# One more k-pair of Down in seven products, and Up's groups twice as wide

## The chip, the cores and the metric

The kernel runs on one core of a Trainium2 chip. The metric is the time of one execution on the device in microseconds (us). Its engines are TensorE (PE in the profile; PEld is its weight load), VectorE (DVE), ScalarE (ACT), GpSimd (POOL) and SyncE (SP), which here only issues transfers. On-chip memory is SBUF; TensorE writes its sums to eight banks of PSUM, each 128 partitions by 512 numbers.

## The reference

One layer of a trunk over 256 tokens of 2048 numbers, all in float32. The part in question is the last one, the feed-forward block:

```
h   = RMSNorm(x)                      # 256 x 2048
u   = h @ w_up                        # 2048 x 11264, called Up here
u   = sum(conv_w[j] * shifted(u, j) for j in range(3)) + conv_b
a,b = split(u, 2, axis=-1)            # 5632 columns each
x   = x + (silu(a) * b) @ w_down      # 5632 x 2048, called Down here
```

Before it stand another norm, the input projection (2048 x 5632), windowed attention, a gated linear recurrence and the output projection.

## The kernel before

**Three products for one.** Each float32 operand is cut in two parts for TensorE: a high part (a cast to fp32r, by ScalarE) and a low part (the operand less its high part, by VectorE). A product of tiles is high x high, high x low and low x high. Every weight therefore passes a transfer, a cast on ScalarE and a subtraction on VectorE before TensorE can use it. The weights move in units of 128 x 1024 numbers through rings of four buffers (`raw`, `w_hi`, `w_lo`); four units are a "quad". `units_split` counts the units that VectorE has finished, `units_used` those that TensorE has used.

**Up.** The 11264 columns are taken in 44 groups of 256, alternately of the a half and the b half (`for g in range(22)`: a, then b). One group is one quad of weights; TensorE runs 64 matmuls for it, 32 of 512 columns and 32 of 256, into two banks (`quad_channels`). While TensorE runs the next group, ScalarE and VectorE work on the last one (`a_work`, `b_work`): VectorE brings it from the banks to `U` (`evacuate`: two reductions and a product with the norm), ScalarE makes the last tap of the convolution (`last_tap`), VectorE the other two (`taps`), ScalarE the silu of an a group; for a b group VectorE forms the product a*b, ScalarE casts it to `gated`, and VectorE subtracts. Between these steps both engines cut the four units of the next quad (`make_hi`, `make_lo`). Everything runs in the order written, on each engine.

**Down.** The 5632 rows of `w_down` are taken as 22 k-pairs of 256 rows, and the 2048 output columns as two column pairs of 1024. One k-pair of one column pair is a product of 2 x 2 blocks, and with two token tiles it takes eight block products, each of three matmuls: 24 matmuls of 512 columns (`four`). Or it takes seven block products, 21 matmuls, by a scheme in the manner of Strassen and Winograd (`seven`). This needs four sums of weight blocks and four sums of activations. The strings in `PATTERNS` say for each column pair which k-pairs are of which kind: S is seven products, C, D and c are eight. The k-pairs of kind S are the first 16 of the activations (`SEVENS`); the order in which they are taken is `SEVEN_ORDER`.

**The sums.** The sums of activations are made in Up, in the work on a b group, for the groups below `SEVENS` (four small additions on VectorE, then two casts and two subtractions). Fourteen of them stay in SBUF; the rest is written from ScalarE's queue to DRAM (`park_sums`) out of one place at the end of `gated`, and brought back in Down (`fetch_sums`). `hi_of_sums(g)` may write that place again only when the transfer before has landed (`sum_parked`). Of the sums of weights two are built in DRAM ahead of time by GpSimd's queue, with transfers that add, at a pace set by `SUM_STEP` and `FIRST_SUM_UNIT` (one step for each 3.5 units used, from unit 20). A third one is either built there too (for the k-pairs in `THIRD_SUM_IN_DRAM`, 5 of 16) or made by VectorE in Down (L1745); the fourth always by VectorE (L1746).

**Buffers in Down.** The first four k-pairs (kind C) still use the ring of Up. From the fifth on, called q4 here (q counts the 44 k-pair turns of Down from 0), the pieces of a k-pair go through slots: 3 large raw slots and a small one (`slots_in_turn`), and two for the high parts (`HI_SLOTS`), so VectorE can be two turns ahead of TensorE at most. A k-pair of kind S has three pieces: a (two blocks), b (three blocks), c (two blocks). VectorE's order per turn is: cut a, form the sums, cut b, cut c. When the sevens of a column pair are done their banks are merged with the output (`free_the_banks`, `rest_of_merge`, `add_last`, all on VectorE).

Of the kernel before, what the change touches and what calls it, by code (L numbers as in the profile page):

```python
# [31 lines left out]
F32 = mybir.dt.float32  # L32
# [35 lines left out]
UP_GROUPS = D_FF // GC  # L68
OUT_GROUPS = D_MODEL // GT
# [12 lines left out]
PATTERNS = ["CCCCSSSSSSSSDSSSSSSSSc", "CcSSSDSSSSSSSDSSSSSSCc"]  # L82
# [6 lines left out]
THIRD_SUM_IN_DRAM = (1, 4, 7, 10, 13)  # L89
LAST_PARKED_TURN = 6  # L90
# [25 lines left out]
SUM_STEP = (7, 2)  # L116
FIRST_SUM_UNIT, SUM_PAUSE = 20, (30, 38)
# [13 lines left out]
def hybrid_layer(nc, x, attn_norm, w_in, q_norm, k_norm, sinks, lb_logits, hg_norm, w_out,  # L131
                 ffn_norm, w_up, conv_w, conv_b, w_down, out):
    ctx = ExitStack()
    with ctx:
# [26 lines left out]
        eps = sb("eps", [P, 1])  # L161
        N_SMALL = 2 * HG_HEADS + 3 + 2 * KT
        N_CONV = 2 * D_FF // P
        cols = sb("cols", [P, N_SMALL + (1 + CONV) * N_CONV])
# [3 lines left out]
        qk_gain = sb("qk_gain", [P, 1])  # L168
        q_eps = sb("q_eps", [P, TT])
        q_scale = sb("q_scale", [P, 2, TT, 2])  # L170
        ss = sb("ss", [P, TT])
        ss_part = sb("ss_part", [P, TT, OUT_GROUPS])
        x_rms_row = sb("x_rms_row", [P, SEQ])
        neg_ss = sb("neg_ss", [P, TT])
        o_ss = sb("o_ss", [P, TT * 2])
# [35 lines left out]
        small = region("small_region", 8448)  # L211
# [9 lines left out]
        C = sb_at(place, "C", [P, 2, 2, SEQ])  # L221
# [168 lines left out]

        bank_x = [bank[4], bank[5], bank[6], bank[7], bank[1], bank[2], bank[3], bank[4]]
# [119 lines left out]
        sums_of = [[bank[4], bank[5], bank[6], bank[7]], [bank[0], bank[1], bank[2], bank[3]]]  # L511
# [25 lines left out]
        SUMS_BACK_AT = [5, 7]  # L537
        X2_BACK_AT = [[5, 14, 17, 20], [13, 15, 17, 19]]
# [17 lines left out]
        def _(sp):  # L556
# [53 lines left out]
            with sp.Fori(0, UP_GROUPS) as g:  # L610
                load_channels(g * 2 + Q_UP, w_up_v, g * GC)
                load_channels(g * 2 + Q_UP + 1, w_up_v, g * GC + D_FF)
# [168 lines left out]
        def _(act):  # L781
# [76 lines left out]
            def spread_row(n):  # L858
                act.wait_ge(row_spread, n + 1)
                act.copy(x_rms_row[:, :], bank[6][:, 0:SEQ]).then_inc(row_made, 1)  # L860
# [234 lines left out]
            make_hi(Q_UP + 1, 3)  # L1095

            def last_tap(n, ab, g):

                act.wait_ge(groups_evacuated, n + BANK_PAIRS + G_UP + 1)
                for c in range(2):  # L1100
                    col = g * 2 + ab * (N_CONV // 2) + c
                    act.activation(C[:, ab, c, :], U[:, c, 2:SEQ + 2], ACT.Identity,  # L1102
                                   scale=cols[:, bass.ds(col + conv_col(2), 1)],
                                   bias=cols[:, bass.ds(col + C_BIAS, 1)]).then_inc(tap2, 1)

            def a_work(g, quad):
                make_hi(quad, 0)
# [1224 lines left out]
```

## Time and profile before

| | us |
|---|---|
| median of 3 runs | 1080.18 (1080.04 to 1081.68) |
| the profiled execution | 1080.29 |
| its span, first to last instruction | 1078.6 |
| around the span | 1.7 |
| Up, by TensorE's rows | 366.9 to 857.1 |
| Down, by TensorE's rows | 857.1 to 1075.2 |

| engine | busy us | share of the span |
|---|---|---|
| PE | 1073.7 | 100% |
| PEld | 928.9 | 86% |
| DVE | 908.6 | 84% |
| ACT | 633.9 | 59% |
| POOL | 79.8 | 7% |

The granted clock of TensorE is 1.00 over the whole span. The page lists busy time and the chain that ended last; the lists by line and shape give mean durations; the timeline gives starts, from which the step from one instruction to the next on an engine can be read. That step can be shorter than the duration, since an instruction begins before the one before it has wholly ended. Times within the span are counted from its start.

### The profile page before, as it was taken

What the parts mean: (1) busy time and instruction counts of PE and PEld (TensorE: products, weight loads), DVE (VectorE), ACT (ScalarE), POOL (GpSimd) and SP (SyncE); (2) the same over time, 40 slices, a digit from 0 to 9 for tenths busy, and PEclk for the clock granted to TensorE, in tenths of its full rate; (3) what the DMA queues carried; (4) which work ended last, traced back from release to release, by engine and by line L of the source; (5) the groups of instructions that cost most, each with busy time, mean ns of one, the idle gap of its engine ahead of it and who ended that gap; (6) DMA issues with size and microseconds to landing.
All of it is one profiled execution on the core that took longest, in us unless ns stands there. A gap on an engine that the chain in (4) does not pass through costs nothing.

```text
span 1078.6 us, 18188 instructions
## 1 busy us (share of the span) xinstructions
PE 1073.7 (100%) x6543; PEld 928.9 (86%) x6543; DVE 908.6 (84%) x1376; ACT 633.9 (59%) x930; POOL 79.8 (7%) x114
## 2 busy tenths in 40 slices
PE   9999999999999999999999999999999999999998
PEld 9888888888888889888888988888888888888887
DVE  7878988889655678888888888888877889999997
ACT  7677676757554655545555555545555566656663
POOL 4500000000000000000000000000000000000000
PEclk9999999999999999999999999999999999999999
DMA  8656687777889888798888888889888789798884
GB/s 275 183 163 176 190 229 223 216 223 222 234 258 245 278 236 235 240 256 239 249 232 243 237 255 245 227 258 247 271 240 235 218 282 319 256 309 315 260 289 163
DMA packets 192336, 260.77 MB, mean 242 GB/s; under 512 B 9605, under 2 KB 143894, under 8 KB 192022
## 3 DMA queue, kind: packets, MB, share of 16 engines
q1 hardware_dynamic: 176246, 216.24, 62.4%
q0 software_dynamic: 13344, 38.80, 17.6%
q10 hardware_dynamic: 2688, 5.00, 1.2%
q8 instruction: 31, 0.51, 0.2%
q14 instruction: 27, 0.22, 0.1%
HBM read 255.02 MB, written 43.78 MB: 277 GB/s over the span
## 4 chain that ended last, share of the span: by engine, by line
PE 99%; DMA 1%; DVE 0%; SPq 0%; issue 0%; DVEq 0%
PE bank L1821 38%; PE bank L1829 20%; PE bank L2216 7%; PE bank L2215 7%; PE bank L2214 7%; PE bank L2067 3%; PE bank L1868 3%; PE bank L2068 3%; PE bank L2069 3%; PE bank L1869 3%; PE bank L1870 3%; PE bank L1789 1%; PE bank L1897 1%; DMA xt<-in_x_dram 1%; PE bank L2106 0%; PE bank L1986 0%
## 5 line engine op out<-in xcount | busy, mean ns | idle before, releaser
L792 ACT CAST w_hi<-raw 128x1024 fp32r<-128x1024 f32 x299 | 311.9, 1048 | 252.7 <-PE bank L1829 118.4
L1201 DVE TENSOR_TENSOR w_lo<-raw,w_hi 128x1024 fp32r<-128x1024 f32 x299 | 363.8, 1222 | 108.1 <-ACT w_hi L792 107.5
L1821 PE MATMUL bank<-hs,w_hi 128*128 128x512 f32 x1792 | 423.0, 391 | 0.0
L1821 PEld LDWEIGHTS bank<-hs,w_hi 128*128 128x128 f32 x1792 | 331.3, 188 | 66.2 <-issue 0.9
L1829 PEld LDWEIGHTS bank<-hs,w_lo 128*128 128x128 f32 x1792 | 224.6, 192 | 5.7 <-issue 0.2
L1829 PE MATMUL bank<-hs,w_lo 128*128 128x256 f32 x1792 | 227.3, 283 | 0.0
L1171 ACT CAST hi_slot<-slot 128x1024 fp32r<-128x1024 f32 (+1 forms) x102 | 117.7, 1187 | 64.7 <-DVE slot L1746 25.2
L1728 DVE TENSOR_TENSOR slot_lo<-slot,hi_slot 128x1024 fp32r<-128x1024 f32 (+1 forms) x102 | 136.7, 1388 | 5.8 <-ACT hi_slot L1171 4.7
L2216 PE MATMUL bank<-hi_slot,gated 128*128 128x512 f32 (+1 forms) x194 | 75.1, 387 | 0.0
L2214 PE MATMUL bank<-hi_slot,gated 128*128 128x512 f32 (+1 forms) x194 | 75.1, 387 | 0.0
L1646 DVE SCALAR_TENSOR_TENSOR C<-U,cols,C 128x256 f32<-128x256 f32 x176 | 73.3, 478 | 0.0
L2215 PE MATMUL bank<-slot_lo,gated 128*128 128x512 f32 (+1 forms) x154 | 59.5, 386 | 0.0
L1102 ACT ACTIVATE C<-U,cols 128x256 f32<-128x256 f32 x88 | 48.1, 594 | 13.2 <-DVE U L1212 13.2
L1868 PE MATMUL bank<-w_hi,mix 128*128 128x512 f32 x128 | 50.3, 393 | 0.0
L2067 PE MATMUL bank<-w_hi,hs 128*128 128x512 f32 x128 | 50.3, 393 | 0.0
L2068 PE MATMUL bank<-w_lo,hs 128*128 128x512 f32 x128 | 49.9, 390 | 0.0
L1870 PE MATMUL bank<-w_hi,mix 128*128 128x512 f32 x128 | 49.9, 390 | 0.0
L1869 PE MATMUL bank<-w_lo,mix 128*128 128x512 f32 x128 | 49.8, 389 | 0.0
L2069 PE MATMUL bank<-w_hi,hs 128*128 128x512 f32 x128 | 49.8, 389 | 0.0
L2214 PEld LDWEIGHTS bank<-hi_slot,gated 128*128 128x128 f32 x194 | 36.4, 188 | 7.5
L2216 PEld LDWEIGHTS bank<-hi_slot,gated 128*128 128x128 f32 x194 | 36.4, 188 | 7.3
L771 POOL DMA_DIRECT2D u_sums<-in_w_ffn_down_dram x21 | 19.3, 918 | 219.9 <-PE bank L1821 92.3
(248 smaller groups left out, 1183.8 us busy)
## 6 DMA issues: line engine op xcount, KB each, us to landing
raw<-in_w_ffn_up_dram SPq DMA_DIRECT2D x176, 512.0 KB, 5.2
u_sums<-in_w_ffn_down_dram POOLq DMA_DIRECT2D x58, 512.0 KB, 6.7
raw<-in_w_in_dram SPq DMA_DIRECT2D x51, 512.0 KB, 4.5
slot<-in_w_ffn_down_dram SPq DMA_DIRECT2D x38, 512.0 KB, 5.0
slot<-u_sums SPq DMA_DIRECT2D x74, 256.0 KB, 5.6
raw<-in_w_in_dram SPq DMA_DIRECT2D x66, 256.0 KB, 4.2
raw<-in_w_out_dram SPq DMA_DIRECT2D x32, 512.0 KB, 5.7
u_sums<-u_sums POOLq DMA_DIRECT2D x16, 512.0 KB, 7.4
```

The costliest lines, as they stand in the source:

```text
L792: act.copy(w_hi[:, i, :], raw[:, i, :]).then_inc(units_hi, 1)
L1171: act.copy(hi_slot(q, piece), raw_of(q, piece)).then_inc(units_hi, 1)
L1201: dve.tensor_tensor(w_lo[:, i, :], raw[:, i, :], w_hi[:, i, :].bitcast(F32), ALU.subtract)\
L1728: dve.tensor_tensor(lo_slot(q, piece), raw_of(q, piece), hi_slot(q, piece).bitcast(F32), ALU.subtract).then_inc(units_split, 1)
L1821: m = pe.matmul(banks[b][:, :], w_hi[:, i, c], hs[:, 4 * i + k, :], start=(first and k == 0), stop=(final and k == 3))
L1829: m = pe.matmul(banks[b][:, 0:SEQ], w_lo[:, i, c], hs[:, 4 * i + k, 0:SEQ], start=False, stop=False)
L1868: pe.matmul(banks[t][:, :], x_hi, hi, start=(k0 + k == 0), stop=False)
L1870: last = pe.matmul(banks[t][:, :], x_lo, hi, start=False, stop=(k0 + k == k_all - 1))
L2067: pe.matmul(o, x_hi, hi, start=(u == 0 and k == 0), stop=False)
L2214: pe.matmul(dst[:, :], x_hi, hi, start=start, stop=False)
L2215: pe.matmul(dst[:, :], x_hi, lo, start=False, stop=False)
L2216: return pe.matmul(dst[:, :], x_lo, hi, start=False, stop=stop)
```

## The change

Up is taken by groups of 512 columns: a 512-wide a group is two quads into four banks (`quad_wide`), then a b group of the same width. The work on them by VectorE and ScalarE stays in pieces of 256: a, a, b, b. One more quad than before is cut ahead of the first work (`Q_UP + 2`), and each piece of work is interleaved with the quad `work + Q_UP + 3`. The last b group is still taken by 256 columns each. The loops of ScalarE and VectorE are written out. A unit of Up's weights is loaded as 2 rows by 512 columns in place of 4 by 256. `C` has three tiles in place of two. `SEVENS` goes from 16 to 17 (34 turns with seven products and 10 with eight, before 32 and 12), nine third sums are built in DRAM before Down in place of five, three sums of activations are parked in place of two, and GpSimd's steps come each 3 units from unit 16.

```
-PATTERNS = ["CCCCSSSSSSSSDSSSSSSSSc", "CcSSSDSSSSSSSDSSSSSSCc"]
+PATTERNS = ["CCCCSSSSSSSSSSSSSSSSSc", "CcSSSSSSSSSDSSSSSSSSCc"]
-THIRD_SUM_IN_DRAM = (1, 4, 7, 10, 13)
-LAST_PARKED_TURN = 6
+THIRD_SUM_IN_DRAM = tuple(range(0, 17, 2))
+LAST_PARKED_TURN = 8
-SUM_STEP = (7, 2)
-FIRST_SUM_UNIT, SUM_PAUSE = 20, (30, 38)
+SUM_STEP = (3, 1)
+FIRST_SUM_UNIT, SUM_PAUSE = 16, (30, 38)
...
+            def load_wide(n, ab):
+                for half in range(2):
+                    for i in range(RING):
+                        load_unit(n * 4 + Q_UP + 2 * ab + half, i, w_up_v, 8 * half + 2 * i, 2, n * GT + ab * D_FF, GT)
...
+            for n in range(UP_PAIRS):                       # ScalarE
+                for g in (2 * n, 2 * n + 1):
+                    a_work(g, 2 * n + g)
+                    if g - 1 in range(RESIDENT_SUMS, SEVENS) and g % 2 == 0:
+                        park_sums(g - 1)
+                for g in (2 * n, 2 * n + 1):
+                    if g == UP_GROUPS - 1:
+                        act.wait_ge(sum_parked, 16 * PARKED_SUMS)
+                    b_work(g, 2 * n + g + 2)
+                    if g - 1 in range(RESIDENT_SUMS, SEVENS) and g % 2 == 1:
+                        park_sums(g - 1)
+                    if g < SEVENS:
+                        hi_of_sums(g)
...
+            for n in range(UP_PAIRS):                       # VectorE
+                for g in (2 * n, 2 * n + 1):
+                    a_work(g, 2 * n + g)
+                for g in (2 * n, 2 * n + 1):
+                    b_work(g, 2 * n + g + 2)
+                    if g < SEVENS:
+                        lo_of_sums(g)
...
+            with pe.Fori(1, UP_PAIRS - 1) as n:
+                for ab in range(2):
+                    pe.wait_ge(groups_evacuated, n * 4 + 2 * ab + G_UP)
+                    for half in range(2):
+                        quad_wide(n * 4 + 2 * ab + half + Q_UP, half, banks_up[ab])
+            pe.wait_ge(groups_evacuated, (UP_PAIRS - 1) * 4 + G_UP)
+            for half in range(2):
+                quad_wide(Q_DOWN - 4 + half, half, banks_up[0])
+            pe.wait_ge(groups_evacuated, (UP_PAIRS - 1) * 4 + 2 + G_UP)
+            for half in range(2):
+                quad_channels(Q_DOWN - 2 + half, banks_up[1][half])
```

**The end of Up on VectorE.** Before, the work on the last b group is interleaved with the last four units of the ring (`w_lo`), and the first piece for a slot (`slot_lo`) follows the last of them:

```order
L1212 TENSOR_TENSOR U<-U,x_rms_row 128x2x256
L1201 TENSOR_TENSOR w_lo<-raw,w_hi 128x1024
L1646 SCALAR_TENSOR_TENSOR C<-U,cols,C 128x256 x4
L1201 TENSOR_TENSOR w_lo<-raw,w_hi 128x1024
L1662 TENSOR_TENSOR C<-C 128x512
L1201 TENSOR_TENSOR w_lo<-raw,w_hi 128x1024
L1665 TENSOR_TENSOR gated<-C,gated 128x2x256
L1201 TENSOR_TENSOR w_lo<-raw,w_hi 128x1024
L1728 TENSOR_TENSOR slot_lo<-slot_116,hi_slot_126 128x1024
```

In the changed kernel, from the product of the last b group but one on (the same place by the units of the ring):

```order
L1691 TENSOR_TENSOR C<-C 128x512
L1221 TENSOR_TENSOR w_lo<-raw,w_hi 128x1024
L1694 TENSOR_TENSOR gated<-C,gated 128x2x256
L1221 TENSOR_TENSOR w_lo<-raw,w_hi 128x1024
L1228 TENSOR_REDUCE U<-bank 128x256
L1229 TENSOR_REDUCE U<-bank 128x256
L1232 TENSOR_TENSOR U<-U,x_rms_row 128x2x256
L1675 SCALAR_TENSOR_TENSOR C<-U,cols,C 128x256 x4
L1691 TENSOR_TENSOR C<-C 128x512
L1694 TENSOR_TENSOR gated<-C,gated 128x2x256
L1755 TENSOR_TENSOR slot_lo<-slot_116,hi_slot_126 128x1024
L1773 TENSOR_TENSOR slot_116<-slot_116 128x512
```

A whole group's work now stands between the last unit of the ring and the first piece of a slot, with no unit among its steps.

**The first parked sum on ScalarE.** Before, behind the silu of the a group of 15: the transfer of sum 14 is issued, and the casts of sum 15 (`gated<-C 128x128` and `128x384`) follow a whole b group later:

```order
L1113 ACTIVATE C<-C 128x512
L792 CAST w_hi<-raw 128x1024 x2
L1139 DMA s_parked<-gated 128x2x384
L792 CAST w_hi<-raw 128x1024
L1102 ACTIVATE C<-U,cols 128x256 x2
L792 CAST w_hi<-raw 128x1024 x2
L1123 CAST gated<-C 128x2x256
L792 CAST w_hi<-raw 128x1024
L1134 CAST gated<-C 128x128
L1135 CAST gated<-C 128x384
```

In the changed kernel, at the end of the work on the b group of 15:

```order
L1115 ACTIVATE C<-U,cols 128x256 x2
L803 CAST w_hi<-raw 128x1024 x2
L1143 CAST gated<-C 128x2x256
L803 CAST w_hi<-raw 128x1024
L1159 DMA s_parked<-gated 128x2x384
L1154 CAST gated<-C 128x128
L1155 CAST gated<-C 128x384
L803 CAST w_hi<-raw 128x1024
```

The two casts, which wait until the transfer has landed, now stand right behind its issue.

## Rows read from the trace of the kernel before

**Rows 1.** The page: busy time by engine, and the chain that ended last.

```profile
PE 1073.7 (100%) x6543; PEld 928.9 (86%) x6543; DVE 908.6 (84%) x1376; ACT 633.9 (59%) x930; POOL 79.8 (7%) x114
...
PE 99%; DMA 1%; DVE 0%; SPq 0%; issue 0%; DVEq 0%
```

**Rows 2.** The waits of TensorE: line, whom for, us in total, times, longest.

```profile
PE bank L1794 <- DVE all_mean L1265: 1.1, 1, 1.1
PE bank L1789 <- DMA xt<-in_x_dram: 0.2, 1, 0.2
```

**Rows 3.** Timeline of TensorE in Down: start us, duration us, engine, line, operation.

```profile
857.16 0.39 PE L2214 MATMUL bank<-w_hi,gated 128*128 128x512 f32 x1
...
878.92 0.39 PE L2214 MATMUL bank<-hi_slot,s_hi 128*128 128x512 f32 x1
...
913.60 0.39 PE L2214 MATMUL bank<-hi_slot,gated 128*128 128x512 f32 x1
```

**Rows 4.** Timeline of VectorE, end of Up's work and begin of Down's.

```profile
859.64 0.68 DVE L1208 TENSOR_REDUCE U<-bank 128x256 f32<-128x512 f32 x1
...
860.96 0.69 DVE L1212 TENSOR_TENSOR U<-U,x_rms_row 128x512 f32<-128x512 f32 x1
...
862.70 1.66 DVE L1646 SCALAR_TENSOR_TENSOR C<-U,cols,C 128x256 f32<-128x256 f32 x4
...
867.81 0.68 DVE L1665 TENSOR_TENSOR gated<-C,gated 128x512 fp32r<-128x512 f32 x1
869.38 1.22 DVE L1201 TENSOR_TENSOR w_lo<-raw,w_hi 128x1024 fp32r<-128x1024 f32 x1 [0.89 <-ACT w_hi L792]
870.52 1.22 DVE L1728 TENSOR_TENSOR slot_lo<-slot,hi_slot 128x1024 fp32r<-128x1024 f32 x1
```

**Rows 5.** Timeline of ScalarE in the same stretch.

```profile
861.68 1.10 ACT L1102 ACTIVATE C<-U,cols 128x256 f32<-128x256 f32 x2 [0.47 <-DVE U L1212]
...
866.53 0.62 ACT L1123 CAST gated<-C 128x512 fp32r<-128x512 f32 x1
868.30 1.05 ACT L792 CAST w_hi<-raw 128x1024 fp32r<-128x1024 f32 x1 [1.15 <-PE bank L2216]
```

**Rows 6.** Timeline of VectorE in a run of sevens, and in the second column pair.

```profile
905.59 4.03 DVE L1728 TENSOR_TENSOR slot_lo<-slot,hi_slot 128x1536 fp32r<-128x1536 f32 x3
909.54 0.68 DVE L1745 TENSOR_TENSOR slot<-slot 128x512 f32<-128x512 f32 x1
910.14 0.68 DVE L1746 TENSOR_TENSOR slot<-slot 128x512 f32<-128x512 f32 x1
910.86 2.90 DVE L1728 TENSOR_TENSOR slot_lo<-slot,hi_slot 128x1536 fp32r<-128x1536 f32 x2
...
918.39 4.03 DVE L1728 TENSOR_TENSOR slot_lo<-slot,hi_slot 128x1536 fp32r<-128x1536 f32 x3
922.35 0.68 DVE L1746 TENSOR_TENSOR slot<-slot 128x512 f32<-128x512 f32 x1
923.07 4.03 DVE L1728 TENSOR_TENSOR slot_lo<-slot,hi_slot 128x1536 fp32r<-128x1536 f32 x3
...
974.87 4.03 DVE L1728 TENSOR_TENSOR slot_lo<-slot,hi_slot 128x1536 fp32r<-128x1536 f32 x3
```

**Rows 7.** Groups by line and shape in Down (858 to 1079): busy us, mean ns.

```profile
L1728 DVE TENSOR_TENSOR slot_lo<-slot,hi_slot 128x1536 fp32r<-128x1536 f32 x32 | 56.3, 1758 | 2.1 <-ACT hi_slot L1171 1.0
```

**Rows 8.** Timeline of VectorE in a b group's work in Up, and of TensorE beside it.

```profile
570.70 0.68 DVE L1208 TENSOR_REDUCE U<-bank 128x256 f32<-128x512 f32 x1
...
574.13 1.22 DVE L1201 TENSOR_TENSOR w_lo<-raw,w_hi 128x1024 fp32r<-128x1024 f32 x1 [1.43 <-ACT w_hi L792]
...
583.72 0.69 DVE L1208 TENSOR_REDUCE U<-bank 128x256 f32<-128x512 f32 x1
...
564.56 7.44 PE L1821 MATMUL bank<-hs,w_hi 128*128 128x512 f32 x32
...
575.68 7.44 PE L1821 MATMUL bank<-hs,w_hi 128*128 128x512 f32 x32
```

**Rows 9.** Transfers: line of the parked sums (KB each, median us to landing).

```profile
s_parked<-gated ACTq DMA_DIRECT2D x2, 384.0 KB, 5.1
```

**Rows 10.** SP's queue over 280 to 366 (2 KB rows), then 400 to 600 (1 KB): packets, MB, share.

```profile
q1 hardware_dynamic: 9484, 15.78, 57.2%
...
q1 hardware_dynamic: 38226, 37.97, 59.2%
q0 software_dynamic: 3550, 10.58, 26.1%
```

More of the change, by code:

```diff
@@ new lines, in some_hi, with a_work @@
+            def some_hi(quad, units):
+                for i in units:
+                    if quad < Q_DOWN + 2:
+                        make_hi(quad, i)
+            def a_work(g, work):
+                quad = work + Q_UP + 3
+                some_hi(quad, [0])
+                if g > 1:
+                    act.wait_ge(ab_made, g - 1 + FREE)
+                last_tap(work, 2 * (g % 2), 0, g)
+                some_hi(quad, [1])
+                act.wait_ge(tap0, work * 2 + 2)
+                a = C[:, 2 * (g % 2), :, :].rearrange("p c t -> p (c t)")
+                act.activation(a, a, ACT.Silu).then_inc(silu_a, 1)
+                some_hi(quad, [2, 3])
@@ L1634, in _, with some_lo, taps @@
                 make_lo(Q_UP + 1, i)
+            for i in range(RING):
+                make_lo(Q_UP + 2, i)
             dve.wait_ge(row_made, 2)
-            def taps(n, ab, g, quad):
+            def some_lo(quad, units):
+                for i in units:
+                    if quad < Q_DOWN + 2:
+                        make_lo(quad, i)
+            def taps(work, c_tile, ab, g, quad):
                 dst = U[:, :, 2:SEQ + 2]
-                evacuate(G_UP + ab, n, (n + Q_UP + 1) * RING, dst)
-                make_lo(quad, 0)
+                last_narrow = ab == 1 and g == UP_GROUPS - 2
+                evacuate(banks_up[ab][g % 2], work, (Q_UP + 2 * (work // 2) + 2 - last_narrow) * RING, dst)
+                some_lo(quad, [0])
                 for tap, before, after in ((1, tap2, tap1), (0, tap1, tap0)):
@@ L1648, in taps, with a_work @@
                                                  ALU.mult, ALU.add).then_inc(after, 1)
-                make_lo(quad, 1)
-            def a_work(g, quad):
-                taps(g * 2, 0, g, quad)
-                for i in range(2, RING):
-                    make_lo(quad, i)
-            def b_work(g, quad, sums_too=False):
-                taps(g * 2 + 1, 1, g, quad)
+                some_lo(quad, [1])
+            def a_work(g, work):
+                taps(work, 2 * (g % 2), 0, g, work + Q_UP + 3)
+                some_lo(work + Q_UP + 3, [2, 3])
```

184 lines of the change are left out of this document (100 added, 84 removed).

## The prediction

> **What bounds the kernel now.** I read the page first: TensorE is busy for all of the span, and the chain that ended last is 99% TensorE [rows 1]. Its waits come to 1.3 us in all, both in the first microseconds [rows 2]. So only two things move the time: the number of matmuls, and a wait of TensorE that is not there today. The second needs a look at how much ahead its suppliers are. In Down the first matmul starts at 857.16 and that of the fifth k-pair (q4, the first seven) at 878.92, 96 matmuls later: 0.2267 us each, with no gap [rows 3]. A turn of seven products is 21 of them, 4.76 us; one of eight is 24, 5.44 us.
>
> VectorE's rhythm in the same stretch is the second thing to see. From the cut of one b piece to the cut of the next it takes 5.27 us where it makes the third sum itself (905.59 to 910.86), and 4.68 us where the sum came from DRAM (918.39 to 923.07) [rows 6]. So in a run of sevens VectorE loses 0.51 us a turn against TensorE, or gains 0.08. It lives on a lead: it is two turns ahead at most, and the turns of eight products (two cuts of 1.14, 2.28 us against 5.44) restore it. How thin the lead becomes: the b piece of q11, the last of the first run of eight sevens, is cut from 910.86 on and takes 1.76 us [rows 6, 7], done at 912.62; the matmul that wants it starts at 913.60 [rows 3]. One microsecond was left, and no wait came of it.
>
> **The change part by part.**
>
> *Fewer matmuls.* 32 x 21 + 12 x 24 = 960 before, 34 x 21 + 10 x 24 = 954 after. Six matmuls of 0.2267 us: **-1.36 us**, all on the path. Up keeps its matmuls. That four banks are used in turn in place of two is not shown by the trace; the nearest rows are Up's own pace (two banks in turn; 32 matmuls of 512 and 32 of 256 in 11.12 us, 564.56 to 575.68 [rows 8]), and Down's, three in a row to the same bank. Of Up's 11.12 us the 512-wide ones take 7.28, so 0.2275 each against 0.2267. I take 0; the bound by these two is 0.0008 x 1408 = 1.1 us, either way.
>
> *The end of Up.* Before, VectorE ends the last unit of the ring at 870.52 and goes straight to q4 [rows 4]. That unit is held by TensorE (ScalarE's cast at 868.30 waits for it [rows 5]), and the order shows the same unit behind the same steps in the changed kernel, so it ends at 870.52 there too. But now the last b group's work comes next, since work lags by one quad more. Its steps, from the rows: two reductions and the product with the norm 859.64 to 861.65, 2.0 us [rows 4]; ScalarE's two taps start then and take 1.10 [rows 5], the four on VectorE follow the first of them and take 1.66 [rows 4], together 2.45; the product a*b, 0.69 and 0.1 of hand-over; ScalarE's cast 0.62 [rows 5] and 0.1; the subtraction 0.68 [rows 4] and 0.1. Sum 6.7 us: VectorE is free at 877.2, ScalarE at 876.5. ScalarE casts q4's piece a (1.05) until 877.5, VectorE cuts it until 878.7, adds the fourth sum (0.72, as from 910.14 to 910.86 [rows 6]; the third is in DRAM for this one) and cuts b from 879.4 to 881.15. The b matmul is due six after 878.92, at 880.28, and its weight load 0.2 before. So TensorE is **1.1 us late** at the very first seven, and VectorE's lead, which was 5 us there, is gone. Before, the b cut of q4 was done at 870.52 + 1.14 + 0.60 + 0.72 + 1.76 = 874.7.
>
> *The run of 17 sevens.* With no lead every turn goes at the slower of the two paces. From q4 to q20 there are 16 steps; by the order of k-pairs (0 to 5, 14, 15, 16, 6 to 13) eight have the third sum in DRAM. VectorE: 8 x 5.27 + 8 x 4.68 = 79.6 us. TensorE: 16 x 4.76 = 76.2. Another **3.4 us**, so 4.5 us late in this column pair with the 1.1; I take 4.4. The four more third sums in DRAM are counted in it: each turn with one saves VectorE 0.59. Bounds: 2.9 if the group's chain is 1.5 us shorter than my sum of steps; 5.5 if hand-overs between engines are 0.2 longer each.
>
> *The second column pair.* Before, the b cut of its first seven ends at 974.87 + 1.76 = 976.6 [rows 6, 7], and the matmul is due at 878.92 + (16 x 21 + 24 + 48 + 6) x 0.2267 = 972.8 + 5.44 = 978.2: 1.6 ahead. The two turns of eight between the runs, with 8 us of merging on VectorE, set this lead anew, so I take the same after. Its first run has nine turns instead of three: up to its eighth turn four slow and three quick ones, 4 x 0.51 - 3 x 0.08 = 1.8 against 1.6 less the weight load's 0.2. **+0.3 us**, bounds 0 and 1.
>
> *The parked sum.* The casts of sum 15 wait for the landing of the transfer issued just before them; before, they came a b group later and waited for nothing. Behind them on ScalarE stands the next quad's first cast, and VectorE waits for them before the next a group. A quad of TensorE is 11.12 us. A b group with sums takes VectorE 13.02 us (570.70 to 583.72), 1.6 of it idle for casts [rows 8]; b groups start 2.5 us into a quad and end 4.4 into the next. The second b in a row has no idle: it ends 4.4 + 11.4 - 11.1 = 4.7 into the next, so the order a, a, b, b costs nothing by itself. Now the parking: ScalarE issues it behind its last cast, 12.6 us into the quad; 5.1 us to land [rows 9] makes 17.7; casts and subtraction 1.35; VectorE ends at 19.05, 7.95 into the next quad instead of 4.7. Then two reductions, product and first unit, 3.15: ready at 11.1 where TensorE's load asks at 10.9; taps and second unit 2.75: ready at 13.85 where it is asked for at 12.7. **+1.1 us**, once; bounds 0 (landing 2 us sooner) and 2. Later parkings have a group between.
>
> The Trainium skill, in "DMA: Bandwidth & Descriptors", section "Anatomy of one DMA — SWDGE (gpsimd) path", puts a transfer (of GpSimd's queue; this one is ScalarE's) at 2.0 us fixed plus its bytes at 436 GB/s. For 384 KB that is an estimate of 2.9 us, where the row of this kernel's own transfer says 5.1 under load; by the page TensorE would not be held in Up and the sum would be 1.1 lower.
>
> *Transfers.* Wider rows make no lighter load: SP's queue moves 15.78 MB in 57.2% of 86 us with 2 KB rows, and 37.97 MB in 59.2% of 200 us with 1 KB rows [rows 10], 0.321 MB per us of full use both times. GpSimd's queue takes 26.1% and gets 3.5/3 of it: 30%, four points more. Before Down is reached a load in Up has 2 to 3 us to spare (5.2 us to landing, a buffer free some 8 us ahead), so 0. In Down the fetch of the parked sums waits for the last `gated`, which comes at 877.2 in place of 868.5 (867.81 + 0.68 [rows 4]), and q6's loads queue behind it on SP. VectorE wants them at 887. I take 0; upper bound 1.5.
>
> **Sum.** 1080.29 (the profiled execution, 0.11 above the median of its kernel) - 1.36 + 4.4 + 0.3 + 1.1 = **1084.7 us**. Range of this case alone: 1082.8 to 1087.
>
> **The rivals.**
>
> *Not slower: the lead survives.* If VectorE cuts q4's b by 876.8 (880.28 less 0.2 for the load less the run's 3.4), TensorE never waits, and 1080.29 - 1.36 is left, 1078.9 to 1080.0 with or without the parked sum. It decides at one point: the time at which VectorE comes to its first `slot_lo`, 873.2 instead of my 877.5. For it: before, VectorE had 5 us of lead there, and my chain is a sum of steps, not a row. Against it: the engine runs in order, and the group's work stands whole in front. 13%. With Up also at the pace of Down's matmuls it would be 1077.8: 3%.
>
> *Half of it.* The chain is 2 to 3 us shorter, or the steps of the run overlap better: 1081.3 to 1082.8. 8%.
>
> *The parking lands early.* If the transfer takes under 3.5 us where it now stands (other queues idle for a moment), the first b group's end moves back and TensorE isn't held in Up: 1084.7 - 1.1 = 1083.6. The row of the same transfer speaks against it. 6%. That is what the Trainium skill's fixed cost in "DMA: Bandwidth & Descriptors" would make of it.
>
> *Transfers become the bound.* 8 more third sums, two more sevens and a larger fetch are 3.4 MB more in Down, and in Up GpSimd's share rises. If q6 to q8 come 2 to 5 us late, or loads in Up do, 1086.5 to 1090. For it: SP's queue will be near 90% in Down's run. Against it: VectorE's slower pace lowers the demand. 12%.
>
> The forecast itself has 58%. A difference below 0.2% can't be told from no change in this kernel; 0.2% is 2.2 us, so slower means above 1082.3. From the cases: slower 0.79, same 0.18, faster 0.03. The range from 1081.0 to 1088.5 leaves out the surviving lead and the worst of the transfers.
>
> **What the profile after would show.** Right: waits of TensorE on VectorE's cuts, in turns with L1772 above all, about 4.4 us of them between 880 and 961; the first `slot_lo` at 877 to 878 (plus what Up lost); one wait of about 1 us in Up at the b group of 15; some 0.3 in the second pair; fours unchanged; TensorE's mean step without waits still 0.2267. Wrong: no wait of TensorE in Down (then the chain is short or VectorE is ahead for another reason), waits on casts that wait for transfers, or a changed pace in Up.

## The result, and the profile of the changed kernel

The changed kernel took **1084.7 us** (median of 6 runs, 1082.97 to 1085.64), the kernel before 1080.16 us beside it. The ratio is 1.0038, with a 95% interval of 1.0027 to 1.005: slower by 0.4%. The profiled execution took 1084.34 us, with a span of 1082.6 against 1078.6.

The page first: busy time and instructions of each engine, then two rows of the chain that ended last (to set beside [rows 1]).

```profile
PE 1076.6 (99%) x6537; PEld 927.0 (86%) x6537; DVE 910.9 (84%) x1380; ACT 636.7 (59%) x934; POOL 88.5 (8%) x126
...
PE 91%; DVE 5%; issue 2%; DMA 2%; ACT 0%; SPq 0%; DVEq 0%
```

TensorE has 6 matmuls fewer, yet is busy for longer in the sum, and the chain is no longer TensorE's alone: VectorE has 5% of it. Whom TensorE waited for (us in total, times, longest), the answer to [rows 2]:

```profile
PE bank L2291 <- DVE slot_lo L1755: 1.4, 4, 0.7
PE bank L1821 <- DVE all_mean L1285: 1.1, 1, 1.1
```

The second row is the old wait in the first microseconds. The first one is new: in Down, TensorE waits for VectorE's cuts (`slot_lo`). The view counts 1.4 us, and that is too little, since the end of a matmul is modelled. The starts tell more. TensorE in Down (start, duration, engine and line, operation, out<-in, and in brackets the idle time before and who ended it), to set beside [rows 3]:

```profile
879.12 0.40 PE L2291 MATMUL bank<-hi_slot,s_hi 128*128 128x512 f32 x1
...
880.27 0.39 PE L2293 MATMUL bank<-hi_slot,s_lo 128*128 128x512 f32 x1
881.33 0.50 PE L2291 MATMUL bank<-hi_slot,gated 128*128 128x512 f32 x1 [0.67 <-DVE slot_lo L1755]
881.66 0.40 PE L2292 MATMUL bank<-slot_lo,gated 128*128 128x512 f32 x1
881.90 0.40 PE L2293 MATMUL bank<-hi_slot,gated 128*128 128x512 f32 x1
...
886.60 0.50 PE L2291 MATMUL bank<-hi_slot,gated 128*128 128x512 f32 x1 [0.19 <-DVE slot_lo L1755]
...
964.73 0.40 PE L2291 MATMUL bank<-hi_slot,gated 128*128 128x512 f32 x1
```

From 880.27 to 881.33 is 1.06 us where 0.227 would do, and the step behind it is 0.33: 0.94 us lost, of which the bracket shows 0.67. Steps of this kind stand at ten places between 881 and 961. The whole loss can be read without them: 879.12 is the 97th matmul of Down, the first one of the sevens, and 964.73 is the 454th. Those 357 steps at 0.2267 us are 80.93 us, and they took 85.61: **4.68 us late** over the run. In the trace of before the same two stand at 878.92 and 959.92, 0.07 late.

With these starts the span adds up. The last matmul starts at 1079.45, and before at 1074.90: 4.55 later. Of that 0.20 was there when the sevens began, 4.61 came in the run of the first column pair, six matmuls fewer give back 1.36, and the second column pair adds 1.10. What lies behind the last matmul took 3.2 us in place of 3.7, so the span is 4.0 longer. (It is 3.2 in every profile with the wide Up and 3.6 to 3.7 in every one with Up by single groups; what shortened it, no run was made to show.)

The end of Up and the start of Down on VectorE, the answer to [rows 4]:

```profile
873.45 1.77 DVE L1675 SCALAR_TENSOR_TENSOR C<-U,cols,C 128x256 f32<-128x256 f32 x4 [0.73 <-ACT C L1115]
875.33 0.69 DVE L1691 TENSOR_TENSOR C<-C 128x512 f32<-128x512 f32 x1
876.71 0.69 DVE L1694 TENSOR_TENSOR gated<-C,gated 128x512 fp32r<-128x512 f32 x1 [0.69 <-ACT gated L1143]
877.66 1.23 DVE L1755 TENSOR_TENSOR slot_lo<-slot,hi_slot 128x1024 fp32r<-128x1024 f32 x1 [0.26 <-ACT hi_slot L1191]
878.80 0.68 DVE L1773 TENSOR_TENSOR slot<-slot 128x512 f32<-128x512 f32 x1
879.52 4.03 DVE L1755 TENSOR_TENSOR slot_lo<-slot,hi_slot 128x1536 fp32r<-128x1536 f32 x3
```

VectorE comes to the first `slot_lo` at 877.66, where it came at 870.52. From there on it has hardly any idle time until the run is over, and TensorE is always the one that waits.

### The profile page after: what moved, and what is told of

It is laid out like the page before. It is cut to its first block, busy times and chain, and to the rows that moved or that the text cites. A ratio compares the mean times of both kernels' runs of the same rounds, so it can differ in the third digit from the quotient of the medians.

```text
span 1082.6 us, 17898 instructions
## 1 busy us (share of the span) xinstructions
PE 1076.6 (99%) x6537; PEld 927.0 (86%) x6537; DVE 910.9 (84%) x1380; ACT 636.7 (59%) x934; POOL 88.5 (8%) x126
## 4 chain that ended last, share of the span: by engine, by line
PE 91%; DVE 5%; issue 2%; DMA 2%; ACT 0%; SPq 0%; DVEq 0%
PE bank L1877 28%; PE bank L1885 15%; PE bank L1848 10%; PE bank L1856 5%; PE bank L2291 4%; PE bank L2293 4%; PE bank L2292 4%; DVE slot_lo L1755 4%; PE bank L2136 3%; PE bank L1937 3%; PE bank L1939 3%; PE bank L2138 3%; PE bank L2137 3%; PE bank L1938 3%; DMA slot<-u_sums 2%
## 5 line engine op out<-in xcount | busy, mean ns | idle before, releaser
L1191 ACT CAST hi_slot<-slot 128x1024 fp32r<-128x1024 f32 (+1 forms) x108 | 122.7, 1186 | 62.1 <-DVE slot L1773 42.6
L1755 DVE TENSOR_TENSOR slot_lo<-slot,hi_slot 128x1024 fp32r<-128x1024 f32 (+1 forms) x108 | 144.5, 1388 | 4.7 <-ACT hi_slot L1191 3.5
L2291 PE MATMUL bank<-hi_slot,gated 128*128 128x512 f32 (+1 forms) x186 | 73.4, 395 | 1.9 <-DVE slot_lo L1755 1.4
L2293 PE MATMUL bank<-hi_slot,gated 128*128 128x512 f32 (+1 forms) x186 | 72.1, 388 | 0.0
L2292 PE MATMUL bank<-slot_lo,gated 128*128 128x512 f32 (+1 forms) x162 | 62.8, 387 | 0.0
L2136 PE MATMUL bank<-w_hi,hs 128*128 128x512 f32 x128 | 50.3, 393 | 0.0
```

The source lines that it names most:

```text
L1191: act.copy(hi_slot(q, piece), raw_of(q, piece)).then_inc(units_hi, 1)
L1755: dve.tensor_tensor(lo_slot(q, piece), raw_of(q, piece), hi_slot(q, piece).bitcast(F32), ALU.subtract).then_inc(units_split, 1)
L2291: pe.matmul(dst[:, :], x_hi, hi, start=start, stop=False)
L2292: pe.matmul(dst[:, :], x_hi, lo, start=False, stop=False)
L2293: return pe.matmul(dst[:, :], x_lo, hi, start=False, stop=stop)
```

## The experiments

Times are medians; each has the kernel before measured beside it on the same chip (1080.1 to 1080.2 us each time). "Late in the run" is the number from above: start of the 454th matmul of Down less that of the 97th, less 80.93 us. "Sevens begin" is the start of the 97th. Both are from the one profiled execution.

| kernel | us, median (lowest to highest) | ratio, 95% interval | profiled | sevens begin | late in the run |
|---|---|---|---|---|---|
| before | 1080.16 | | 1080.29 | 878.92 | 0.07 |
| changed | 1084.7 (1082.97-1085.64) | 1.0038 (1.0027-1.005) | 1084.34 | 879.12 | 4.68 |
| wide Up alone | 1083.98 (1083.49-1087.34) | 1.0041 (1.0027-1.0056) | 1084.27 | 879.39 | 4.02 |
| Down alone | 1079.5 (1078.72-1080.78) | 0.9995 (0.9985-1.0004) | 1080.64 | 879.19 | 0.59 |
| changed, all third sums | 1083.27 (1081.43-1087.42) | 1.003 (1.002-1.004) | 1084.74 | 883.00 | 1.64 |
| changed, park later | 1086.41 (1085.76-1090.09) | 1.0067 (1.0048-1.0086) | 1086.18 | 881.66 | 4.38 |
| changed, first seven early | 1083.72 (1082.56-1084.92) | 1.003 (1.0019-1.0041) | 1084.23 | 879.62 | 4.04 |
| changed, park early | 1083.77 (1083.39-1084.52) | 1.0033 (1.0021-1.0045) | 1083.85 | 878.98 | 4.66 |
| both moves | 1082.74 (1082.35-1083.31) | 1.0022 (1.0013-1.0031) | 1082.70 | 878.86 | 4.13 |
| both moves, fetch later | 1081.14 (1080.44-1081.6) | 1.0008 (0.9999-1.0017) | 1080.86 | 878.77 | 2.32 |
| the same, 12 third sums | 1079.57 (1078.97-1082.16) | 0.9997 (0.9988-1.0006) | 1079.56 | 878.72 | 0.73 |
| changed, fetch later | 1083.81 (1083.39-1084.68) | 1.0033 (1.0021-1.0046) | 1083.39 | 879.42 | 4.34 |
| Down alone, all third sums | 1079.93 (1079.03-1083.3) | 1.0001 (0.9992-1.001) | 1083.30 | 881.88 | 0.08 |
| Down alone, 12 third sums | 1080.41 (1079.57-1081.6) | 1.0002 (0.9993-1.0011) | 1079.57 | 878.66 | 0.08 |

### One half of the change at a time

The changed kernel with Down as it was before:

```diff
-PATTERNS = ["CCCCSSSSSSSSSSSSSSSSSc", "CcSSSSSSSSSDSSSSSSSSCc"]
+PATTERNS = ["CCCCSSSSSSSSDSSSSSSSSc", "CcSSSDSSSSSSSDSSSSSSCc"]
-THIRD_SUM_IN_DRAM = tuple(range(0, 17, 2))
-LAST_PARKED_TURN = 8
+THIRD_SUM_IN_DRAM = (1, 4, 7, 10, 13)
+LAST_PARKED_TURN = 6
-SUM_STEP = (3, 1)
-FIRST_SUM_UNIT, SUM_PAUSE = 16, (30, 38)
+SUM_STEP = (7, 2)
+FIRST_SUM_UNIT, SUM_PAUSE = 20, (30, 38)
...
-        SUMS_BACK_AT = [5, 6]
-        X2_BACK_AT = [[15, 17, 19, 20], [14, 16, 18, 19]]
+        SUMS_BACK_AT = [5, 7]
+        X2_BACK_AT = [[5, 14, 17, 20], [13, 15, 17, 19]]
```

> The changed Up (512-wide groups, the work lagging by one quad more) with the Down of before: 16 k-pairs in seven products, five third sums in DRAM, GpSimd's old pace. TensorE has the matmuls of before, so 1080.2 us plus waits. Theory 1 (the last group's work stands ahead of the first piece of a slot and takes VectorE's lead): the first seven makes its third sum itself, so its b cut is done at 881.9, 1.8 us late with the weight load; the first run of eight sevens (six slow turns, two quick) adds 2.4; the D turn then gives 3 us of lead and nothing more is lost: 4.2 us, 1084.4 us, all of it between 880 and 916. Theory 2 (the longer run of sevens is what costs, not Up): no wait beyond the run of eight that was covered before, 1080.2 us.

The last four lines are the turns at which the parked sums and the parked parts of `x` come back on SyncE's queue. The other half is the kernel before with these lines turned round, and with the changed kernel's layout of its small tensors: its Up by single groups, and 17 sevens.

> The Up of before with the changed Down: 17 k-pairs in seven products, nine third sums in DRAM, three parked sums, GpSimd's new pace. Theory 1: VectorE comes to its first slot at 870.5 with some 4 us of lead, the run of 17 uses 3.0 of the 3.8 that the two slots for high parts allow, or all of it where third sums land late: waits of 0 to 0.7 us in the first pair and 0.3 to 1 in the second, less 1.36 for six matmuls: 1079.6 us (1078.9 to 1080.6). Theory 2 (the run itself is too long): waits of 3 to 4 us there too, 1082 to 1084 us.

Up alone took 1083.98 us, 3.9 over before, and Down alone 1079.5, 0.6 under it (its interval includes no change). So most of the loss comes with Up's wide groups, though it is paid in Down. The two halves add up to 3.3 of the 4.5 us; the rest shows only with both together. The start of the sevens on VectorE, first with the wide Up alone, then with Down alone:

```profile
876.97 0.69 DVE L1694 TENSOR_TENSOR gated<-C,gated 128x512 fp32r<-128x512 f32 x1 [0.69 <-ACT gated L1143]
877.93 1.23 DVE L1755 TENSOR_TENSOR slot_lo<-slot,hi_slot 128x1024 fp32r<-128x1024 f32 x1 [0.26 <-ACT hi_slot L1191]
```

```profile
869.64 1.23 DVE L1199 TENSOR_TENSOR w_lo<-raw,w_hi 128x1024 fp32r<-128x1024 f32 x1 [0.89 <-ACT w_hi L790]
870.79 1.22 DVE L1726 TENSOR_TENSOR slot_lo<-slot,hi_slot 128x1024 fp32r<-128x1024 f32 x1
```

The 17 sevens with nine third sums cost 0.59 us of lateness where VectorE starts 7 us sooner, and 4.68 where it doesn't. The old pattern, with an eight between the sevens, doesn't save it either: late start and old pattern give 4.02. In the first column pair the lead at the start decides, and not the number of sevens.

### All third sums in DRAM

```diff
-THIRD_SUM_IN_DRAM = tuple(range(0, 17, 2))
+THIRD_SUM_IN_DRAM = tuple(range(17))
-SUM_STEP = (3, 1)
+SUM_STEP = (5, 2)
```

> The changed kernel with all 17 third sums built in DRAM (nine before) and GpSimd's steps each 2.5 units. VectorE then takes 4.68 us for each turn of a run where TensorE takes 4.76. If VectorE is what holds TensorE in the run, only the 1.1 us at the first seven stay: some 1081 us (1080 to 1082). If the transfers are the bound (SP's queue near 90%), 16 more of 256 KB in Down and eight more builds of 512 KB in Up make it slower than the changed kernel: over 1085 us.

Lateness in the run fell from 4.68 to 1.64 us, as it should if VectorE's own pace makes most of it. What stays is the late start (1.0 us at 885) and one more wait, at 895.30, where VectorE waited for casts that themselves had waited for loads. So transfers are not what the run of sevens waits for in the changed kernel. The median fell by 1.4 only. The profiled execution lost time ahead of Down: its sevens begin at 883.00. ScalarE and TensorE in that trace:

```profile
745.99 0.37 ACTq L1159 DMA_DIRECT2D s_parked<-gated  x1
746.02 1.05 ACT L803 CAST w_hi<-raw 128x1024 fp32r<-128x1024 f32 x1
754.70 0.30 ACT L1154 CAST gated<-C 128x128 fp32r<-128x128 f32 x1 [7.64 <-DMA s_parked<-gated]
```

```profile
754.79 2.20 PE L1877 MATMUL bank<-hs,w_hi 128*128 128x512 f32 x9
759.33 5.68 PE L1877 MATMUL bank<-hs,w_hi 128*128 128x512 f32 x16 [2.34 <-DVE w_lo L1221]
```

The parked sum landed after 8.7 us in this execution, and TensorE stood for 2.3 us. The 16 matmuls behind it then lasted 5.68 us, 0.35 each where 0.227 would do. The granted clock explains that. Stretches in and behind the wait (length; busy time of PE, PEld, DVE, ACT and POOL with their instructions; granted clock; DMA share; GB/s):

```profile
757.00:759.30 2.30, 0.00 (x0) 0.00 (x0) 2.27 (x4) 1.07 (x3) 0.92 (x1) 1.00 0.00 2
...
761.00:762.00 1.00, 1.00 (x3) 0.33 (x1) 0.99 (x1) 1.00 (x2) 0.00 (x0) 0.50 1.13 170
762.00:763.00 1.00, 1.00 (x3) 0.83 (x3) 0.51 (x1) 1.00 (x2) 0.00 (x0) 0.50 1.15 172
...
764.00:765.00 1.00, 1.00 (x7) 0.83 (x6) 1.00 (x2) 0.00 (x0) 0.00 (x0) 1.00 0.85 264
```

Some three microseconds at half the clock (1.2 GHz in place of 2.4) add 1.7 us to the 2.6 lost by the wait itself. That one late transfer ate most of what the sums in DRAM gave this execution. For the median it shows less: over the whole span two of the ten executions have a granted clock of 0.998, this one and the slowest, and the others 1.000. What those lost, no trace shows.

### The parked sum, later and earlier

In the changed kernel's profile this place cost 0.1 us, not the 1.1 that I had reckoned. ScalarE there:

```profile
746.37 0.37 ACTq L1159 DMA_DIRECT2D s_parked<-gated  x1
746.38 1.05 ACT L803 CAST w_hi<-raw 128x1024 fp32r<-128x1024 f32 x1
751.68 0.30 ACT L1154 CAST gated<-C 128x128 fp32r<-128x128 f32 x1 [4.25 <-DMA s_parked<-gated]
```

The transfer goes out at 746.37, while the cast that stands ahead of it in the program only starts at 746.38. I had put the issue behind that cast's end. One kernel holds it back until then, by a wait on a count that the cast raises:

```diff
                 if g == RESIDENT_SUMS:
+                    act.wait_ge(units_hi, (Q_UP + 35) * RING)
```

> The changed kernel, but the first parked sum's transfer is issued only when ScalarE's cast in front of it has ended (a wait on that cast's count), as the prediction had assumed. In the changed kernel it went out 1.1 us earlier, with the cast still running, and TensorE lost 0.1 us in Up. If the step failed in that term alone, VectorE's next a group comes 1.1 us later and TensorE waits 0.3 to 1.1 us around 757 to 760: 1085.4 us. If the parking has slack that the prediction did not see, TensorE waits no more than 0.2 us there and the time is 1084.7.

It took 1086.41 us, 1.7 more than the changed kernel. The issue moved by 0.8 us, but in its profile the landing also took 7.0 us and not 5.3, and TensorE lost 3.0 us at two places:

```profile
758.84 2.11 PE L1879 MATMUL bank<-hs,w_hi 128*128 128x512 f32 x8 [1.81 <-DVE w_lo L1223]
761.56 1.66 PE L1879 MATMUL bank<-hs,w_hi 128*128 128x512 f32 x6 [0.61 <-DVE w_lo L1223]
```

Direction right, size too small: I had moved the issue only, and the landing is not constant.

The other kernel sends the sum of seven 14 right behind its own casts, one group sooner:

```diff
                 for g in (2 * n, 2 * n + 1):
                     a_work(g, 2 * n + g)
-                    if g - 1 in range(RESIDENT_SUMS, SEVENS) and g % 2 == 0:
+                    if g - 1 in range(RESIDENT_SUMS + 1, SEVENS) and g % 2 == 0:
                         park_sums(g - 1)
...
                     if g < SEVENS:
                         hi_of_sums(g)
+                    if g == RESIDENT_SUMS:
+                        park_sums(g)
```

> The changed kernel, with one transfer moved: the sum of seven 14 goes to DRAM right behind its own casts, a group of Up sooner, so that the slot that it leaves has some 12 us more before a cast writes it. Theory 1, the median of the changed kernel holds some part for this transfer's landing, which varied between 4 and 9 us over the profiles: no TensorE wait in Up, the median 1084.0 or lower, and the runs closer together (1083.5 to 1084.3). Theory 2, it lands in time in nearly all executions: 1084.7 and the spread of 1083 to 1085.6 as before.

```profile
739.47 0.37 ACTq L1159 DMA_DIRECT2D s_parked<-gated  x1
...
748.96 0.30 ACT L1154 CAST gated<-C 128x128 fp32r<-128x128 f32 x1 [1.52 <-DVE C L1714]
```

The cast now waits for its own data, no longer for the transfer. The median is 1083.77, 0.9 lower, and the runs lie within 1.1 us where they lay within 2.7; the lateness in the run of sevens is unchanged (4.66). So the changed kernel's median holds about 0.9 us for this place, although its profiled execution shows 0.1. (With six executions of each, the intervals of the two ratios overlap.) One trace had shown one landing.

### The first seven's work among the last group's steps

```diff
+            def hi_of_first(piece):
+                q = OLD_RING
+                wait_for_down(act, q, piece)
+                act.wait_ge(units_split, {"a": LAST_OLD - 3, "b": LAST_OLD - 1}[piece] + 1 + RING)
+                act.copy(hi_slot(q, piece), raw_of(q, piece)).then_inc(units_hi, 1)
...
+            def split_first(piece):
+                q = OLD_RING
+                dve.wait_ge(units_hi, piece_number(q, piece) + 1)
+                dve.tensor_tensor(lo_slot(q, piece), raw_of(q, piece), hi_slot(q, piece).bitcast(F32),
+                                  ALU.subtract).then_inc(units_split, 1)
```

The first is called on ScalarE inside the last b group's work (piece a ahead of its taps, b behind them), the second on VectorE ahead of the four taps; the fourth sum follows the product.

> The changed kernel with its two-wide Up groups and its 17 sevens as they are. Only one thing moves: the work of Down's first seven on ScalarE and VectorE (cast and difference of its a piece, its fourth sum, cast of its b piece) stands among the steps of Up's last b group, in the idle times there, and no longer behind them. VectorE is then ready with that seven some 1.9 us sooner (1.23 of the a difference and 0.68 of the sum leave the tail). Theory 1, the late chain at the end of Up sets the lateness of the first column pair: its 4.1 us of TensorE waits fall to about 2.3, the time to about 1082.9. Theory 2, the place of that chain doesn't matter and VectorE's rate in the run of sevens alone makes the waits: 1084.7, waits in the first pair still about 4.

1083.72 us: 1.0 lower, not 1.8. Its own profile had a slow landing of the parked sum (0.98 us lost in Up), so the run is read better in the next one, which has both moves.

> Both of the moves before it: the first seven's work among the steps of the last b group, and the sum of seven 14 sent to DRAM a group sooner. The first theories of both: 4.1 us of waits in the first column pair fall to 2.3, none is left in Up: 1082.2. If neither place matters: 1084.7.

1082.74 us, 0.5 over the expectation. The run is 4.13 late, not 2.3. VectorE and ScalarE:

```profile
877.28 4.02 DVE L1787 TENSOR_TENSOR slot_lo<-slot,hi_slot 128x1536 fp32r<-128x1536 f32 x3
...
886.49 1.23 DVE L1787 TENSOR_TENSOR slot_lo<-slot,hi_slot 128x1024 fp32r<-128x1024 f32 x1 [1.05 <-ACT hi_slot L1205]
```

```profile
885.40 1.05 ACT L1205 CAST hi_slot<-slot 128x1024 fp32r<-128x1024 f32 x1 [1.81 <-DMA slot<-in_w_ffn_down_dram]
887.39 3.39 ACT L1205 CAST hi_slot<-slot 128x1536 fp32r<-128x1536 f32 x3 [0.94 <-DMA slot<-u_sums]
```

The move did what it should: VectorE cuts the b piece of the first seven from 877.28 on, and in the changed kernel from 879.52, 2.2 us later. But at 885 ScalarE stands and waits for weights. The gain turned into a wait for transfers. Why these come late is seen on SyncE's queue, in the same trace:

```profile
865.46 0.47 SPq L672 DMA_DIRECT2D slot<-u_sums  x1
877.39 0.33 SPq L631 DMA_DIRECT2D parked_sums<-s_parked  x1
877.76 0.43 SPq L666 DMA_DIRECT2D slot<-u_sums  x1
```

The fetch of the parked sums waits for the last b group's product (11.4 us, by the view of SyncE's waits), and the next seven's weights stand behind it in the queue.

### The fetch behind two more loads

```diff
-        SUMS_BACK_AT = [5, 6]
+        SUMS_BACK_AT = [7, 6]
```

With both moves, and then in the changed kernel alone:

> The run with both moves (first seven's work among the steps of the last b group, sum of seven 14 sent a group sooner; it took 1082.7 us), and the fetch of the parked sums stands on SyncE's queue behind the loads of the eighth k-pair of the first column pair, not behind those of the sixth. In that run SyncE waited 11.4 us, to 877.4, for the last b group's product in front of this fetch, and the weights of the next seven went out only behind it, at 877.8; ScalarE then waited 1.8 and 0.9 us for Down's weights and TensorE lost 1.6 us at 890 to 897. Theory 1, this queue position is what ate most of the gain that the earlier chain should have brought: the loads go out by 871, the 1.6 us fall to 0.3 or less and some 2.1 us, the run's own rate, stay: 1081.3. Theory 2, the slots come free no sooner or the transfers are slow themselves: 1082.7.

> The changed kernel with one thing moved: the fetch of the parked sums stands on SyncE's queue behind the loads of the eighth k-pair of the first column pair, not behind those of the sixth. The chain at the end of Up and the parking stay as they were. Theory 1, in the first column pair two things are late one behind the other, VectorE by its chain and the weights by this queue position, and each covers most of the other: alone the fetch gives only what ScalarE waited for weights at 886 and 888 (0.65 and 0.66 us in the changed kernel's trace), so 0 to 0.7 us, 1084.4, while with the chain out of the way the same move gave 1.6 us (1082.74 to 1081.14). Theory 2, the queue position is the main cause and the chain is not: the waits up to 897 (2.1 us) go, 1083.0 or lower.

With both moves the loads go out at 870.81, and ScalarE waits for no weights:

```profile
870.81 0.33 SPq L666 DMA_DIRECT2D slot<-u_sums  x1
...
883.36 0.38 SPq L631 DMA_DIRECT2D parked_sums<-s_parked  x1
```

```profile
882.45 3.38 ACT L1205 CAST hi_slot<-slot 128x1024 fp32r<-128x1024 f32 x3 [2.54 <-DVE slot L1805]
887.11 3.38 ACT L1205 CAST hi_slot<-slot 128x1024 fp32r<-128x1024 f32 x3 [1.28 <-DVE slot L1805]
```

1081.14 us, 1.6 lower, against 1081.3 expected; the run is 2.32 late. Four traces form a square (three of them with the early parking, "only the fetch moved" without it). Chain late and fetch early 4.66, only the fetch moved 4.34, only the chain moved 4.13, both moved 2.32. By the run of sevens each alone gives 0.3 to 0.5, the two together 2.3. Two things were late one behind the other, and each covered part of the other. By the medians it is less sharp: the chain alone gives 1.0 (1083.77 to 1082.74), the fetch alone 0.9, and both 2.6 (1083.77 to 1081.14). So the two together give more than their sum in both measures, by 1.5 us in single traces and by 0.7 in medians that are known to some tenths.

In the changed kernel alone the same line gave 1083.81, 0.9 lower. That is more than the 0.3 expected of the first theory and less than the 1.7 of the second. The run's part is the 0.3; in the profiles the second column pair lost 1.0 us less, and Up 0.4 more, than in the changed kernel, which one execution of each can't tell from chance.

### More third sums

The run with both moves and the later fetch, and third sums for 12 sevens; then the kernel before with Down's 17 sevens, all third sums in DRAM, and 12 of them:

```diff
-THIRD_SUM_IN_DRAM = tuple(range(0, 17, 2))
+THIRD_SUM_IN_DRAM = (0, 2, 3, 4, 6, 7, 8, 10, 11, 12, 14, 16)
-SUM_STEP = (3, 1)
+SUM_STEP = (14, 5)
```

> The run before it and the third sum in DRAM for 12 of 17 sevens, not nine. Theory: with the chain at the end of Up, the parked sum and the fetch out of the way, what is left is VectorE's rate in the run of sevens; three sums fewer a column pair give back 1.8 us at most: 1080.0, and 1079.0 if no wait is left at all. Rival: the waits are now the transfers', and more of them doesn't help: 1081.3 or more.

> The kernel before with its Up by single groups as it was, and of the change only Down: 17 sevens a column pair, but with the third sum in DRAM for all 17 of them instead of nine, 128 KB more for each of eight sevens. That takes 8 x 0.60 us of sums from VectorE in each column pair. Theory 1, VectorE is what the run of sevens waits for: the 0.43 and 0.85 us of waits that the same kernel with nine third sums showed go, and 6 matmuls fewer at 0.2267 us give 1080.1 - 1.4 = 1078.7. Theory 2, the transfers of Down are full with nine: the weights come late, 1079.5 or more, with TensorE waits that end on a DMA.

> The kernel before with its Up by single groups, and Down with 17 sevens a column pair and the third sum in DRAM for 12 of them (k-pairs 0, 2, 3, 4, 6, 7, 8, 10, 11, 12, 14, 16), between the nine and the 17 of the runs before it. Theory: two limits that pull against each other. Sums in DRAM take 0.60 us each from VectorE in Down, and cost transfers in the stages in front, where the run with all 17 showed a TensorE wait of 1.65 us on a weight load and executions that fall into two groups, near 1079.7 and 1083.2. With 12 the waits in Down should be under 0.4 us and the DMA share in the middle some 0.02 under that of all 17, so no upper group: 1079.0 us, 0.1% under the kernel before. Rival: any sum beyond nine brings the upper group: a median like before's or higher, and single runs at 1083.

The first took 1079.57 us: it gave back 1.6 of the 2.3 us, three sums of 0.60 a column pair, as reckoned. That is the changed kernel with all it lost regained, 5.1 us below it, and level with before (0.9997, interval 0.9988 to 1.0006).

Down alone with all third sums has no lateness in the first run of sevens (0.08), and yet a median of 1079.93. Eight of its executions lie between 1079.0 and 1080.4 and three at 1083.2 to 1083.3. The profiled one was of the upper three. Its sevens begin 3.0 us later than before's, and 1.8 of that was lost at one place, in Up, 400 us ahead of Down; the rest is 0.6 near 276 and small steps between 430 and 460. The place on ScalarE and on TensorE:

```profile
464.09 1.05 ACT L790 CAST w_hi<-raw 128x1024 fp32r<-128x1024 f32 x1 [3.70 <-DMA raw<-in_w_ffn_up_dram]
```

```profile
466.45 1.22 PE L1827 MATMUL bank<-hs,w_lo 128*128 128x256 f32 x8 [1.50 <-DVE w_lo L1199]
```

One stretch of Up, first of this kernel, then of before (columns as above; the one before the last is the DMA share):

```profile
700.00:800.00 100.00, 100.00 (x578) 88.55 (x577) 84.63 (x126) 53.91 (x71) 10.49 (x15) 1.00 0.98 282
```

```profile
700.00:800.00 100.00, 100.00 (x577) 88.61 (x576) 83.02 (x120) 52.07 (x68) 7.27 (x10) 1.00 0.89 253
```

Making the sums in DRAM fills the transfers, 0.98 against 0.89, and in this execution a weight load came late. That the one brings the other is likely, but no run shows it by itself. With 12 sums no execution was near 1083, as expected, but the median was 1080.41 and not 1079.0. Its profiled execution was its fastest; it shows no lateness in the first run and 1.0 us more than before in the second column pair. What the slower ones lost, no trace shows; this stays open. No version tried is clearly faster than the kernel before.

## Why the prediction was right

The time, 1084.7, was met to the decimal, and that is partly luck; the steps are what count. In the profiled execution, 0.4 under the forecast, four errors nearly cancel: the parked sum 1.0 less than forecast, the end behind the last matmul 0.5 less, the second column pair 0.8 more and the first run 0.2 more. The mechanism that was forecast, VectorE's lead used up at the end of Up and then its slower pace in the run of sevens, is the one that the runs show.

- **Six matmuls fewer, -1.36.** Right. Between waits the step is 0.227 in both kernels, and Up kept its pace: the sevens begin 0.2 us later than before, against a bound of 1.1.
- **The end of Up, first `slot_lo` at 877.5.** It came at 877.66, and TensorE lost 0.94 us at the first seven, where 1.1 was forecast. The chain was added up from rows of before for each step, with the hand-overs between engines, and it held. The rival in which the lead survives needed 873.2; when the place is undone (Down alone, 870.79) the loss is gone.
- **The run of 17 sevens, +3.4 behind it.** 4.68 less 0.94 is 3.7. All third sums in DRAM brought the run down to 1.64, three more of them from 2.32 to 0.73: VectorE's pace it is. The sum of 4.4 was 0.3 low: the gaps alone come to 4.1, and the other 0.5 is steps of 0.23 to 0.24 us, most of them behind a wait, which I had not counted.
- **The second column pair, +0.3.** Measured 1.1 in the profile, 0.1 over my upper bound. The lead at its start was as I took it, and a little more: the b piece of its first seven is cut from 978.64 on, which ends 2.0 us ahead of its matmul, against 1.6 before. It went in the run, where VectorE stood for 1.0 us in all behind loads, at its own third sum (L1772) and at two cuts whose casts had waited for loads of weights and of their sums:

```profile
978.64 4.03 DVE L1755 TENSOR_TENSOR slot_lo<-slot,hi_slot 128x1536 fp32r<-128x1536 f32 x3
...
1003.34 0.69 DVE L1772 TENSOR_TENSOR slot<-slot 128x512 f32<-128x512 f32 x1 [0.47 <-DMA slot<-u_sums]
```

```profile
1000.56 1.05 ACT L1191 CAST hi_slot<-slot 128x1024 fp32r<-128x1024 f32 x1 [1.00 <-DMA slot<-in_w_ffn_down_dram]
```

  The step that failed is the 0 for transfers in this run. By the same reckoning the loss was 0.1 to 0.8 in the other kernels with the wide Up and 17 sevens, but for one with 1.1, and 0.9 to 1.4 with Down alone. So it comes with Down's new pattern, and the wide Up isn't needed for it. Whether the second fetch of the parked sums, which went out at 991.15, delays these loads was not tested.
- **The parked sum, +1.1.** The size came out near, and the working was wrong. The changed kernel's profiled execution lost 0.1, since the transfer goes out a cast sooner than "behind its last cast, 12.6 us into the quad". The landing that ScalarE waits for, which I took as 5.1 us, lay between 4.1 and 8.7 in the traces. The two errors offset each other, which is luck, and the early parking shows about 0.9 us in the median. The rule of the Trainium skill in "DMA: Bandwidth & Descriptors", section "Anatomy of one DMA — SWDGE (gpsimd) path", is for transfers of GpSimd's queue. Its estimate of 2.9 us for 384 KB doesn't fit this one of ScalarE's queue under load: no landing of a parked sum in any of the traces was below 3.5 us.
- **Transfers, 0.** Nearly right for the changed kernel (moving the fetch gives its run 0.3), and wrong as a reading of what is next. I had seen that the weights queue behind the fetch on SyncE, and wrote that VectorE wants them at 887; they were late by little only because VectorE was late as well. With VectorE 2.2 us sooner this queue position cost 1.8 in the run of sevens, and 1.6 in the median.

## What to carry to other kernels

Before widening a stage's groups, look at who works on its last group when the next stage's first operands are due: here the work that lags one group more was added whole to the chain at the border (7.1 us on VectorE), and a following stage in which the supplier is slower than the consumer doesn't regain it. Price such a run as the supplier's lead at its start against its deficit a turn, here 0.51 us where it makes a sum itself. When a repair gives less than its chain was late by, look for the next thing that is late at the same place before giving up the theory: two repairs that took 0.3 and 0.5 us of lateness alone took 2.3 together (0.9 and 1.0 against 2.6 by the medians).

## What the runs showed of the hardware

- ScalarE's queue sent a transfer out ahead of the end, even of the start, of a cast that stands before it in the program: 746.37 against 746.38 to 747.43. With a wait on that cast's count it went out at 747.19, when the cast was done. So a transfer without such a wait can't be reckoned from the end of the instruction ahead of it.
- The landing of one and the same 384 KB transfer, the one that ScalarE waits for, varied from 4.1 to 8.7 us between the profiled executions of kernels that differ little there, at nearly the same moment of the program. The kernel whose cast waits for it varied by 2.7 us over six executions, and the one without that wait by 1.1 over six.
- A wait of TensorE can cost more than itself. After 2.3 us of standing still and 1.2 us of matmuls at 1.00, the granted clock was 0.50 (1.2 GHz) from about 760.5 to 763.9, and the matmuls there stepped at 0.43 to 0.6 us: 1.7 us on top. Behind the waits under 1 us in Down the clock shows 1.00, and what is lost beside the gaps is only the steps of 0.23 to 0.24 us: 0.5 us over ten waits. Nor were a 1.5 us wait in Up, at 466.45, and the 1.8 us wait of the later parking followed by another clock than 1.00.
